# Norms of a one-core fp32 transformer kernel done by halves of the channels, with the first products ordered by high parts

## The chip, the cores and the metric

The kernel is one program on one core of a Trainium2 chip. The metric is the device time of that core in microseconds. The kernel before takes 1885.22 us in the median of 3 runs (1884.35 to 1890.95).

## The reference

Three transformer blocks follow each other on x of 256 tokens by 1024 channels, all in fp32. What matters here:

```python
def rms_norm_2(x, g):
    y = xf * lax.rsqrt(jnp.mean(xf * xf, axis=-1, keepdims=True) + NORM_EPS)
    return (y * g).astype(x.dtype)

def swiglu(x, w_gate, w_up, w_down):
    return (jax.nn.silu(x @ w_gate) * (x @ w_up)) @ w_down

# first block: hybrid mixer ("proj", "w_out"), then a mixture of experts ("moe"), then a final norm
h = h + hybrid_mixer(rms_norm(h, norm1_g), ...)
h = h + hier_moe(rms_norm(h, norm2_g), ...)
x = rms_norm(h, final_norm_g)
# second block, two layers
for layer in range(2):
    x = x + 0.5 * rms_norm_2(swiglu(rms_norm_2(x, g[0]), ...), g[1])    # ffn0, ffn2
    m = mixer_ab(rms_norm_2(x, g[2]), ...) if layer == 0 else mixer_c(rms_norm_2(x, g[2]), ...)
    x = x + rms_norm_2(m, g[3])
    x = x + 0.5 * rms_norm_2(swiglu(rms_norm_2(x, g[4]), ...), g[5])    # ffn1, ffn3
```

## The kernel before, in words

The 256 tokens are two tiles (t = 0 and 1) of 128. All weights come as a stream of 1 MB units through a ring of 5 buffers, loaded by SyncE. A product in full precision is made of three in TensorE's fast fp32 form: the operands are split into a high part and a low part, and high by high, high by low and low by high are summed. ScalarE makes the high part of a weight unit (L814, `split`), VectorE subtracts it to get the low part (L1305, `split`); a wait on `w_lo` holds TensorE until then.

Between two stages stands a norm, for each tile of tokens. For the norm after a stage and the one before the next:

- ScalarE sums the squares of the stage's result in PSUM (L833, L839), GpSimd turns the sums into rp (L723, L715, L716), VectorE multiplies the result by its gain (L1335) and forms the new row X (L1344; L1323 and L1316, L1317 after the mixture of experts).
- F is X times the next gain (L1358). For the stages in `SCALED` (proj, ab, c) it is also multiplied by rn (L1356), for which ScalarE sums the squares of X (L869, `pre_sums`) and GpSimd takes the power (L715, L716). The FFNs apply rn later, in the silu (L1077) and its product (L1798).
- TensorE turns F by 8 transposes a tile (L2186, `x_turn`), ScalarE copies them as the high part h_hi (L882; L880 for ab), VectorE subtracts for the low part h_lo (L1369), and for c also copies them plainly into H (L1372). Each is two instructions, one for each half of the channels.
- The first products: L2633 to L2635 for an FFN (`gate_up`, 24 for a tile, 12 for each weight unit), L2210 for c (`split_tokens`, 24 for a tile and unit), L2716 for ab.

The order of the work is written out by hand on each engine. In an FFN `gate_up(0, 0)` is followed by the turns of tile 1 and `gate_up(0, 1)`; then come the steps s = 1 to 10, each needing two more gate and up units and, one step behind, a down unit. For s = 0 a product waits for h_lo of its half of the channels:

```python
if s == 0:
    pe.wait_ge(S("h_lo"), HI0[name] + 2 * t + j + 1)
for k in range(4):
    pe.matmul(bank[4 + t][:, :], x_hi, w[0][:, k, :], start=first, stop=False)
    pe.matmul(bank[4 + t][:, :], x_hi, w[1][:, k, :], start=False, stop=False)
    ins = pe.matmul(bank[4 + t][:, :], x_lo, w[0][:, k, :], start=False, stop=end)
```

The turns of an FFN's tiles go to PSUM banks 4, 5 and 6, 7 (`turn_bank`); `gate_up` writes banks 4 and 5, the sums of a stage are banks 0 to 3. ffn1 and ffn3 follow a square product (L2951, L2448), in which the turns of tile 0 stand between its quarters. For c, `split_tokens` of two units is done for tile 0, then tile 1; `keep_busy(n)` are n products of constants whose result is not used (L2255; each leaves two records).

## Time and profile before

| | |
|---|---|
| median of 3 runs | 1885.22 us (1884.35 to 1890.95) |
| the profiled execution | 1885.83 us |
| its span | 1884.0 us |
| TensorE busy | 1829.6 us, 97% of the span, 10816 products |
| VectorE busy | 1176.7 us, 62% |
| ScalarE busy | 887.3 us, 47% |
| GpSimd busy | 49.9 us, 3% |
| mean granted TensorE clock | 0.988 of full speed |
| DMA | 363.58 MB, mean 193 GB/s |

The span is what the profile's rows lie in; the execution's time is 1.8 us longer. In the profile's rows PE is TensorE, DVE VectorE, ACT ScalarE, POOL GpSimd, SP SyncE, and L12 is line 12 of the kernel before. The stages lie at these times of the span: proj from 0, the w_out and moe norm at 341 to 362, the experts to 745, ffn0's start at 749 to 763, ab at 936 to 957, ffn1 at 1126 to 1157, ffn2 at 1321 to 1338, c at 1512 to 1545, ffn3 at 1676 to 1707, the last norm at 1871 to 1882.

### The profile page before, as it was taken

To read this page: it belongs to the slowest core of one execution; us is meant where nothing else is said; L and a number is where in the kernel's file an instruction comes from. 1 tells how busy PE (TensorE), PEld (TensorE's weight loads), DVE (VectorE), ACT (ScalarE), POOL (GpSimd) and SP (SyncE) were. 2 spreads that over 40 slices of the span, in tenths; PEclk is the share of its full clock that TensorE was granted. 3 is DMA by queue.
4 is the path that set the end of the run, shared out by engine and by line. 5 is a ranking of instruction groups with operands and counts; after the bars stand their busy time and mean duration, and the time that the engine had idled before them with its cause. 6 is when DMAs were issued, how large, how long until landed. Compare 5 with 4: busy or idle time off the path is not lost.

```text
span 1884.0 us, 25827 instructions
## 1 busy us (share of the span) xinstructions
PE 1829.6 (97%) x10816; PEld 1568.6 (83%) x10816; DVE 1176.7 (62%) x1458; ACT 887.3 (47%) x1091; POOL 49.9 (3%) x107
## 2 busy tenths in 40 slices
PE   7999999999999999999999999999999999999998
PEld 7998889878888887788888898888788889887887
DVE  5345666479898898645468966554645456745454
ACT  4433442367777675544323245444444345535442
POOL 0030000000000000000000000000000010000000
PEclk9989999999999999999999999999999999999999
DMA  8342334479899888555333007544555534226540
GB/s 353 135 157 90 113 112 180 174 291 363 329 351 343 340 338 323 186 193 201 134 116 131 25 3 294 195 177 182 203 190 176 191 135 152 96 98 248 187 176 39
DMA packets 51523, 363.58 MB, mean 193 GB/s; under 512 B 5712, under 2 KB 5840, under 8 KB 8784
## 3 DMA queue, kind: packets, MB, share of 16 engines
q1 hardware_dynamic: 51264, 359.83, 51.3%
q8 instruction: 86, 1.41, 0.3%
q10 hardware_dynamic: 144, 2.10, 0.3%
q14 instruction: 29, 0.24, 0.0%
HBM read 360.86 MB, written 1.05 MB: 192 GB/s over the span
## 4 chain that ended last, share of the span: by engine, by line
PE 87%; DVE 7%; ACT 4%; issue 2%; POOL 0%; DMA 0%; DVEq 0%; SPq 0%; POOLq 0%; ACTq 0%
PE bank L2633 8%; PE bank L2635 8%; PE bank L2634 8%; PE bank L2171 7%; PE bank L2660 4%; PE bank L2658 4%; PE bank L2659 4%; PE bank L2225 4%; PE bank L2525 3%; PE bank L2527 3%; PE bank L2526 3%; PE bank L2210 3%; PE bank L2448 3%; PE bank L2356 3%; PE bank L2540 2%
## 5 line engine op out<-in xcount | busy, mean ns | idle before, releaser
L1305 DVE TENSOR_TENSOR w_a<-ring,w_a 128x2048 fp32r<-128x2048 f32 x221 | 504.2, 2290 | 277.2 <-ACT w_a L814 276.3
L814 ACT ACTIVATE w_a<-ring 128x2048 fp32r<-128x2048 f32 x221 | 420.2, 1912 | 188.2 <-PE bank L2660 90.1
L2633 PE MATMUL bank<-w_a,h 128*128 128x512 f32 x536 | 212.7, 397 | 6.0 <-DVE h L1369 6.0
L2635 PE MATMUL bank<-w_a,h 128*128 128x512 f32 x536 | 209.2, 390 | 0.0
L2634 PE MATMUL bank<-w_a,h 128*128 128x512 f32 x536 | 208.7, 389 | 0.0
L1305 DVE TENSOR_TENSOR w_b<-ring,w_b 128x2048 fp32r<-128x2048 f32 x62 | 142.0, 2291 | 67.8 <-ACT w_b L814 67.1
L2171 PE MATMUL bank<-h,w_a 128*128 128x256 f32 x1088 | 145.8, 289 | 0.7 <-DVE w_a L1305 0.7
L2171 PEld LDWEIGHTS bank<-h,w_a 128*128 128x128 f32 x1088 | 137.8, 196 | 3.5 <-issue 3.2
L814 ACT ACTIVATE w_b<-ring 128x2048 fp32r<-128x2048 f32 x62 | 118.6, 1914 | 45.7 <-PE bank L2660 25.7
L1077 ACT ACTIVATE sil<-bank,tiny 128x256 f32<-128x256 f32 x88 | 41.8, 475 | 175.2 <-PE bank L2635 175.2
L2633 PEld LDWEIGHTS bank<-w_a,h 128*128 128x128 f32 x536 | 100.7, 188 | 27.1 <-DVE h L1369 4.9
L2635 PEld LDWEIGHTS bank<-w_a,h 128*128 128x128 f32 x536 | 100.6, 188 | 21.5
L2634 PEld LDWEIGHTS bank<-w_a,h 128*128 128x128 f32 x536 | 100.8, 188 | 20.0
L2658 PE MATMUL bank<-w_a,hid 128*128 128x512 f32 x264 | 103.2, 391 | 0.0
L2660 PE MATMUL bank<-w_a,hid 128*128 128x512 f32 x264 | 102.8, 389 | 0.0
L2659 PE MATMUL bank<-w_a,hid 128*128 128x512 f32 x264 | 102.7, 389 | 0.0
L2525 PE MATMUL bank<-w_a,xg 128*128 128x512 f32 x244 | 97.9, 401 | 0.9 <-DVE xg L1680 0.9
L2527 PE MATMUL bank<-w_a,xg 128*128 128x512 f32 x244 | 96.0, 393 | 0.0
L2526 PE MATMUL bank<-w_a,xg 128*128 128x512 f32 x244 | 95.7, 392 | 0.0
L800 ACT ACTIVATE arena<-bank 128x512 f32<-128x512 f32 (+2 forms) x51 | 29.1, 571 | 140.6 <-PE bank L2171 56.9
L1798 DVE SCALAR_TENSOR_TENSOR hid<-bank,tiny,sil 128x256 f32<-128x256 f32 x88 | 42.3, 480 | 73.5 <-ACT sil L1077 73.5
L2210 PE MATMUL bank<-w_a,h 128*128 128x256 f32 x672 | 84.5, 287 | 1.4 <-DVE h L1369 1.4
(473 smaller groups left out, 3277.1 us busy)
## 6 DMA issues: line engine op xcount, KB each, us to landing
ring<-in_stream SPq DMA_DIRECT2D x330, 1024.0 KB, 4.9
G<-in_gains SPq DMA_DIRECT2D x15, 512.0 KB, 5.7
cmp_area<-in_cmp_w ACTq DMA_DIRECT2D x1, 2048.0 KB, 10.9
sm<-in_small SPq DMA_DIRECT2D x1, 1582.0 KB, 13.1
con<-in_consts SPq DMA_DIRECT2D x1, 1032.0 KB, 17.1
X<-in_x SPq DMA_DIRECT2D x2, 512.0 KB, 4.9
out_x<-X SPq DMA_DIRECT2D x4, 256.0 KB, 2.0
sm<-in_small SPq DMA_DIRECT2D x1, 730.5 KB, 23.5
```

What stands on the lines that cost most here:

```text
L814: act.activation(w_slot(unit)[:, 0, :], ring[:, unit % RING, :], ACT.Copy).then_inc(S("w_hi"), 1)
L1305: dve.tensor_tensor(w_slot(unit)[:, 1, :], ring[:, unit % RING, :], w_slot(unit)[:, 0, :].bitcast(FP32), ALU.subtract).then_inc(S("w_lo"), 1)
L2171: ins = pe.matmul(ps, w(wp, k), xp[:, k, :], start=(a == 0 and k == 0), stop=(a == 2 and k == terms - 1))
L2525: pe.matmul(bank[4][:, :], x_hi, w[0][:, k, :], start=(half == 0 and k == 0), stop=False)
L2526: pe.matmul(bank[4][:, :], x_hi, w[1][:, k, :], start=False, stop=False)
L2527: ins = pe.matmul(bank[4][:, :], x_lo, w[0][:, k, :], start=False, stop=(half == 1 and k == 3))
L2633: pe.matmul(bank[4 + t][:, :], x_hi, w[0][:, k, :], start=first, stop=False)
L2634: pe.matmul(bank[4 + t][:, :], x_hi, w[1][:, k, :], start=False, stop=False)
L2635: ins = pe.matmul(bank[4 + t][:, :], x_lo, w[0][:, k, :], start=False, stop=end)
L2658: pe.matmul(ps, x_hi, w[0][:, f, d], start=(s == 0 and f == 0), stop=False)
L2659: pe.matmul(ps, x_hi, w[1][:, f, d], start=False, stop=False)
L2660: return pe.matmul(ps, x_lo, w[0][:, f, d], start=False, stop=(s == last and f == 1))
```

## The change

1. **F by halves.** F, and for the FFNs X too, are made in two instructions of 512 channels. The counter `hs` counts halves, and `x_turn` waits for each half before its 4 transposes.
2. **High parts first.** In the first step of an FFN the 8 products that need only h_hi come before the 4 that need h_lo; the first wait is for h_hi. In c the first unit of each tile waits likewise.
3. **Banks.** An FFN's turns go to banks 6, 7 (tile 0) and 0, 1 (tile 1).
4. **The third weight unit** of an FFN is split by ScalarE before the copies of tile 1, and the sum of squares of tile 1's X (`pre_sums`) comes after the first silu.
5. **c's norm** has an order of its own on ScalarE and VectorE (`norms_c`); the first unit's low part is made in two halves around F.
6. **Fewer keep-busy products** in c: 4 and 2 instead of 8 and 8.

```diff
@@ turn_bank
+            if name in FFNS:
+                return half if t else 6 + half
             return (4, 7)[half] if name in BY_TILE else 4 + 2 * t + half
@@ SyncE
-                        sp.wait_ge(S("hs"), 2 * NB[name])
+                        sp.wait_ge(S("hs"), 4 * NB[name])
@@ ScalarE: post_sums (squares(name, t) holds the two sums of squares, L833 and L839)
+                if name == "c":
+                    split("c", 0)
+                    squares(name, 0)
+                    pre_sums(name, 0)
+                    squares(name, 1)
+                    turned_in(name, 0)
+                    split("c", 1)
+                    pre_sums(name, 1)
+                    turned_in(name, 1)
+                    return
...
-                    else:
+                    elif t == 0:
                         turned_in(name, t)
                         pre_sums(name, t)
-                    if of and t == 0 and SPLIT_EARLY[name] < 2:
-                        split(of, 1)
+                    else:
+                        split(name, 2)
+                        turned_in(name, t)
@@ ScalarE: gated
-                split(name, 2)
                 silu(0, 0)
+                pre_sums(name, 1)
                 split(name, 3)
@@ VectorE: rows (was the end of sums_in)
+                for half in range(2):
+                    d = slice(512 * half, 512 * half + 512)
+                    ins = dve.scalar_tensor_tensor(X[:, t, d], F[:, t, d], rp[:, t:t + 1], X[:, t, d], ALU.mult, ALU.add)
+                    renewed(name, t, half, ins)
+
+            def renewed(name, t, half, ins):
+                if half == 0:
+                    half_renewed(ins)
+                    dve.wait_ge(S("x_half"), x_halves[0])
+                else:
+                    ins.then_inc(S("x_new"), 1)
+                    dve.wait_ge(S("x_new"), 2 * (NB[name] - 1) + t + 1)
+                gained_half(name, t, half)
+
+            def gained_half(name, t, half):
...
+                if name in SCALED:
+                    if half == 0:
+                        dve.wait_ge(S("rn"), 2 * NB[name] + t + 1)
+                    ins = dve.scalar_tensor_tensor(F[:, t, d], X[:, t, d], rn[:, t:t + 1], G[:, 1, d], ALU.mult, ALU.mult)
+                else:
+                    ins = dve.tensor_tensor(F[:, t, d], X[:, t, d], G[:, 1, d], ALU.mult)
+                ins.then_inc(S("hs"), 1)
@@ VectorE: c
+            def norms_c():
+                post_gain("c", 0)
+                rows("c", 0)
+                split("c", 0, slice(0, UNIT // 2))
+                gained("c", 0)
+                split("c", 0, slice(UNIT // 2, UNIT))
+                low_in("c", 0)
+                post_gain("c", 1)
+                split("c", 1)
+                rows("c", 1)
+                whole_in("c", 0)
+                gained("c", 1)
+                low_in("c", 1)
+                whole_in("c", 1)
@@ TensorE: x_turn
-                pe.wait_ge(S("hs"), 2 * NB[name] + t + 1)
                 for half in range(2):
+                    pe.wait_ge(S("hs"), 4 * NB[name] + 2 * t + half + 1)
@@ TensorE: split_tokens(..., first=False)
+                        if first and a != 1:
+                            pe.wait_ge(S("h_lo" if a else "h_hi"), HI0[name] + 2 * t + 2)
@@ TensorE: gate_up
                         if s == 0:
+                            pe.wait_ge(S("h_hi"), HI0[name] + 2 * t + j + 1)
+                            for k in range(4):
+                                x_hi = h_hi[:, 4 * j + k, t * P:(t + 1) * P]
+                                pe.matmul(bank[4 + t][:, :], x_hi, w[0][:, k, :], start=(j == 0 and k == 0), stop=False)
+                                pe.matmul(bank[4 + t][:, :], x_hi, w[1][:, k, :], start=False, stop=False)
                             pe.wait_ge(S("h_lo"), HI0[name] + 2 * t + j + 1)
-                        for k in range(4):
+                            for k in range(4):
+                                ins = pe.matmul(bank[4 + t][:, :], h_lo[:, 4 * j + k, t * P:(t + 1) * P], w[0][:, k, :],
+                                                start=False, stop=(j == 1 and k == 3))
+                        for k in range(4) if s else ():
@@ TensorE: c
-            pe.wait_ge(S("h_lo"), HI0["c"] + 2)
             for n in range(2):
-                split_tokens(group_begin(f"c{8 + n}"), "c", n, range(0, 1))
-            keep_busy(8)
+                split_tokens(group_begin(f"c{8 + n}"), "c", n, range(0, 1), n == 0)
+            keep_busy(4)
             x_turn("c", 1)
-            keep_busy(8)
-            pe.wait_ge(S("h_lo"), HI0["c"] + 4)
+            keep_busy(2)
             for n in range(2):
-                split_tokens(bank[5 + GI[f"c{8 + n}"] % 2], "c", n, range(1, 2))
+                split_tokens(bank[5 + GI[f"c{8 + n}"] % 2], "c", n, range(1, 2), n == 0)
```

VectorE's order at the norm of c, with the semaphores that each instruction waits for. F<-bank,G is the result times its gain, X<-F,tiny,X the new row, F<-X,tiny,G the row for the turns, w_a<-ring,w_a a low part of weights, h<-bank,h is h_lo, H<-bank the plain copy. Before:

```order
1048 L1344 SCALAR_TENSOR_TENSOR X<-F,tiny,X 128x1024 [waits s_rp,s_fg]
1049 L1305 TENSOR_TENSOR w_a<-ring,w_a 128x2048 [waits s_w_hi,s_x_new]
1050 L1356 SCALAR_TENSOR_TENSOR F<-X,tiny,G 128x1024 [waits s_rn,s_gain1]
1051 L1369 TENSOR_TENSOR h<-bank,h 128x4x128 [waits s_h_hi] x2
1052 L1372 COPY H<-bank 128x4x128 x2
1053 L1305 TENSOR_TENSOR w_a<-ring,w_a 128x2048 [waits s_w_hi]
1054 L1335 TENSOR_TENSOR F<-bank,G 128x512 [waits s_ss_p,s_gain0]
1055 L1335 TENSOR_TENSOR F<-bank,G 128x512 [waits s_ss_p]
1056 L1344 SCALAR_TENSOR_TENSOR X<-F,tiny,X 128x1024 [waits s_rp,s_fg]
1057 L1356 SCALAR_TENSOR_TENSOR F<-X,tiny,G 128x1024 [waits s_rn,s_x_new]
```

The same place in the changed kernel, whose line numbers are its own:

```order
1066 L1382 SCALAR_TENSOR_TENSOR X<-F,tiny,X 128x1024 [waits s_rp,s_fg]
1067 L1322 TENSOR_TENSOR w_a<-ring,w_a 128x1024 [waits s_w_hi,s_x_new]
1068 L1411 SCALAR_TENSOR_TENSOR F<-X,tiny,G 128x512 [waits s_rn,s_gain1,s_dve_chain]
1069 L1411 SCALAR_TENSOR_TENSOR F<-X,tiny,G 128x512
1070 L1322 TENSOR_TENSOR w_a<-ring,w_a 128x1024 [waits s_w_hi]
1071 L1431 TENSOR_TENSOR h<-bank,h 128x4x128 [waits s_h_hi] x2
1072 L1368 TENSOR_TENSOR F<-bank,G 128x512 [waits s_ss_p,s_gain0]
1073 L1368 TENSOR_TENSOR F<-bank,G 128x512 [waits s_ss_p]
1074 L1322 TENSOR_TENSOR w_a<-ring,w_a 128x2048 [waits s_w_hi]
1075 L1382 SCALAR_TENSOR_TENSOR X<-F,tiny,X 128x1024 [waits s_rp,s_fg]
1076 L1436 COPY H<-bank 128x4x128 [waits s_x_new]
1078 L1411 SCALAR_TENSOR_TENSOR F<-X,tiny,G 128x512 [waits s_rn]
```

The low part of the first unit stands in two pieces around F, and the low part of the second unit has moved behind the gain of tile 1; the plain copies of tile 0 have moved behind X of tile 1.

ScalarE at the start of ffn2: sums of squares of the result (junk,tiny<-bank), high parts of the turned rows (h<-bank), sum of squares of X (junk,tiny<-X), high parts of weights (w_a, w_b<-ring), the silu. Before, then changed:

```order
645 L833 ACTIVATE junk,tiny<-bank 128x512 [waits s_half_sums]
646 L839 ACTIVATE junk,tiny<-bank 128x512 [waits s_unit_used]
647 L882 ACTIVATE h<-bank 128x4x128 [waits s_x_turned] x2
648 L869 ACTIVATE junk,tiny<-X 128x1024 [waits s_x_new]
649 L814 ACTIVATE w_b<-ring 128x2048 [waits s_unit_used,s_unit1]
650 L1077 ACTIVATE sil<-bank,tiny 128x256 [waits s_gu_0,s_rn]
```

```order
645 L830 ACTIVATE junk,tiny<-bank 128x512 [waits s_half_sums]
646 L836 ACTIVATE junk,tiny<-bank 128x512 [waits s_unit_used]
647 L816 ACTIVATE w_b<-ring 128x2048 [waits s_unit_used,s_unit1]
648 L899 ACTIVATE h<-bank 128x4x128 [waits s_x_turned] x2
649 L1094 ACTIVATE sil<-bank,tiny 128x256 [waits s_gu_0,s_rn]
650 L886 ACTIVATE junk,tiny<-X 128x1024 [waits s_x_new]
```

The third unit's high part has moved ahead of the copies of tile 1, and the sum of squares of X behind the silu.

## Rows read from the trace of the kernel before

**Rows 1.** The page: busy time of each engine, and the chain that ended last
```profile
PE 1829.6 (97%) x10816; PEld 1568.6 (83%) x10816; DVE 1176.7 (62%) x1458; ACT 887.3 (47%) x1091; POOL 49.9 (3%) x107
...
PE 87%; DVE 7%; ACT 4%; issue 2%; POOL 0%; DMA 0%; DVEq 0%; SPq 0%; POOLq 0%; ACTq 0%
```
**Rows 2.** Waits of TensorE: us in total, times, longest us
```profile
PE bank L2186 <- DVE F L1356: 13.4, 5, 8.3
PE bank L2633 <- DVE h L1369: 6.0, 6, 1.1
```
**Rows 3.** VectorE's instructions: duration ns min/median/max by tile; one by the timeline
```profile
L1358 DVE TENSOR_TENSOR F<-X,G x10: 1224/1225/1227, 342.0 to 1694.7; 128x1024 f32<-128x1024 f32 x10
L1341 DVE SCALAR_TENSOR_TENSOR X<-F,tiny,X x4: 744/748/752, 1874.7 to 1880.8; 128x512 f32<-128x512 f32 x4
...
224.64 0.69 DVE L1576 TENSOR_TENSOR SQ<-SQ,arena 128x512 f32<-128x512 f32 x1
```
**Rows 4.** Timeline, ffn2's start: start us, us, instruction [idle before <-releaser]
```profile
1327.91 1.03 PE L2186 MATMUL bank<-con,F 128*128 128x128 f32 x8
1329.17 1.29 DVE L1369 TENSOR_TENSOR h<-bank,h 128x512 fp32r<-128x512 f32 x2 [1.94 <-ACT h L882]
1330.01 0.47 PE L2633 MATMUL bank<-w_a,h 128*128 128x512 f32 x1 [1.07 <-DVE h L1369]
1333.16 1.28 DVE L1344 SCALAR_TENSOR_TENSOR X<-F,tiny,X 128x1024 f32<-128x1024 f32 x1 [0.52 <-POOL tiny L716]
...
1337.82 0.50 PE L2633 MATMUL bank<-w_a,h 128*128 128x512 f32 x1 [0.98 <-DVE h L1369]
```
**Rows 5.** Timeline, ffn0's tile 1
```profile
762.58 0.50 PE L2633 MATMUL bank<-w_a,h 128*128 128x512 f32 x1 [0.97 <-DVE h L1369]
```
**Rows 6.** Timeline, ffn1's tile 1 and its fourth weight unit
```profile
1145.90 1.09 PE L2186 MATMUL bank<-con,F 128*128 128x128 f32 x8
1147.97 0.50 PE L2633 MATMUL bank<-w_a,h 128*128 128x512 f32 x1 [0.98 <-DVE h L1369]
...
1154.15 2.29 DVE L1305 TENSOR_TENSOR w_b<-ring,w_b 128x2048 fp32r<-128x2048 f32 x1 [0.90 <-ACT w_b L814]
...
1156.49 0.50 PE L2633 MATMUL bank<-w_b,h 128*128 128x512 f32 x1
```
**Rows 7.** Timeline, c's norm and first products
```profile
1515.51 2.29 DVE L1305 TENSOR_TENSOR w_a<-ring,w_a 128x2048 fp32r<-128x2048 f32 x1
1516.75 1.13 POOL L715 TENSOR_SCALAR tiny<-tiny 128x1 f32<-128x1 f32 x1 [2.66 <-ACT junk L869]
...
1519.96 1.97 PE L2186 MATMUL bank<-con,F 128*128 128x128 f32 x8 [2.39 <-DVE F L1356]
1523.34 7.38 PE L2210 MATMUL bank<-w_a,h 128*128 128x256 f32 x48 [1.41 <-DVE h L1369]
...
1530.48 0.22 POOL L715 TENSOR_SCALAR tiny<-tiny 128x1 f32<-128x1 f32 x1 [2.78 <-ACT junk L869]
...
1531.44 1.28 DVE L1356 SCALAR_TENSOR_TENSOR F<-X,tiny,G 128x1024 f32<-128x1024 f32 x1 [2.23 <-POOL tiny L716]
...
1535.45 6.01 PE L2210 MATMUL bank<-w_a,h 128*128 128x256 f32 x48
```
**Rows 8.** Stretches: busy us of PE, PEld, DVE, ACT, POOL; PEclk, DMA share, GB/s
```profile
755.00:765.00 10.00, 8.25 (x39) 6.41 (x38) 4.47 (x6) 4.95 (x7) 2.12 (x5) 1.00 0.32 104
945.00:950.00 5.00, 4.30 (x24) 4.31 (x25) 2.58 (x3) 2.35 (x7) 0.98 (x3) 0.66 0.01 3
1520.00:1526.00 6.00, 4.59 (x20) 4.19 (x21) 4.10 (x5) 4.15 (x7) 0.40 (x1) 0.50 0.32 134
```
**Rows 9.** Timeline, the turns of proj (tile 1), moe (tile 1) and ab (tile 0)
```profile
11.21 1.97 PE L2186 MATMUL bank<-con,F 128*128 128x128 f32 x8 [1.00 <-DVE F L1356]
...
357.96 1.09 PE L2186 MATMUL bank<-con,F 128*128 128x128 f32 x8 [0.41 <-DVE F L1358]
...
943.86 1.09 PE L2186 MATMUL bank<-con,F 128*128 128x128 f32 x8 [1.51 <-DVE F L1356]
```

More of the change, by code:

```diff
@@ L1299, in link, with split, half_renewed @@
                 dve.wait_ge(S("dve_chain"), chain[0])
-            def split(name, n):
+            def split(name, n, part=slice(0, UNIT)):
                 unit = D_UNITS[name] + n
                 dve.wait_ge(S("w_hi"), SPLIT0[name] + n + 1)
-                dve.tensor_tensor(w_slot(unit)[:, 1, :], ring[:, unit % RING, :], w_slot(unit)[:, 0, :].bitcast(FP32),
-                                  ALU.subtract).then_inc(S("w_lo"), 1)
+                ins = dve.tensor_tensor(w_slot(unit)[:, 1, part], ring[:, unit % RING, part], w_slot(unit)[:, 0, part].bitcast(FP32),
+                                        ALU.subtract)
+                if part.stop == UNIT:
+                    ins.then_inc(S("w_lo"), 1)
+                else:
+                    link(ins)
+            x_halves = [0]
+            def half_renewed(ins):
+                x_halves[0] += 1
+                ins.then_inc(S("x_half"), 1)
             def sums_in(name, t):
@@ L1361, in turned_in, with low_in @@
+            def gained(name, t):
+                for half in range(2):
+                    gained_half(name, t, half)
             def turned_in(name, t):
+                if name != "ab":
+                    low_in(name, t)
+            def low_in(name, t):
                 tok = slice(t * P, (t + 1) * P)
@@ L1637, in norms @@
                 for t in range(TT):
[L1638 to L1639 removed]
+                    if of and t < SPLIT_EARLY[name]:
                         split(of, t)
                     sums_in(name, t)
[L1642 to L1643 removed]
                     if name == "moe":
@@ L1647, in norms @@
                     elif name != "end":
-                        gained(name, t)
+                        if name in SCALED:
+                            gained(name, t)
                         turned_in(name, t)
-                    if of and t == 0 and SPLIT_EARLY[name] < 2:
-                        split(of, 1)
             dve.wait_ge(S("merged"), 12)
@@ L2202, in split_channels, with split_tokens @@
                 ins.then_inc(S("unit_used"), 1)
-            def split_tokens(ps, name, n, ts=range(TT)):
+            def split_tokens(ps, name, n, ts=range(TT), first=False):
                 w = split_ready(name, n)
```

83 lines of the change are left out of this document (41 added, 42 removed).

## Prediction

> **What bounds the kernel.** I read the page's shares first: TensorE is busy for 97% of the span and holds 87% of the chain that ended last [rows 1]. So only work that keeps TensorE waiting, or runs it at half clock, is worth anything. The table of waits on TensorE comes next: its largest entries are the two that this change aims at, the transposes waiting for VectorE's gained rows (F), and the first FFN products waiting for the low part h_lo [rows 2]. Together they are some 20 us, 1% of the span, and that caps the change. Then I read the timeline around each norm, and the granted clock beside it. A measurement of this kernel can tell about 0.5% (9.4 us) from no change.
>
> **Prices of pieces.** A 1024-wide F takes 1.225 us, a 512-wide X with its pointer scalar 0.748, and a 512-wide tensor_tensor, which F is without a scalar, 0.69 [rows 3]. A whole X takes 1.28 [rows 4]. So X and F of one tile by halves take 0.75+0.69+0.75+0.69, less some 0.16 for the overlap of the unwaited step, plus two waits on itself of 0.04: about 2.86 against 1.28+0.04+1.22 = 2.54. The last F half ends 0.3 us later than F did, the first half 1.1 us earlier. These sizes are known to 0.1; the range takes 0.2.
>
> **ffn2 (the pattern of all FFN starts).** Tile 0: its 8 transposes start at 1327.91, when the products before them end, h_lo's first half starts at 1329.17 when h_hi's is there, and the first product starts at 1330.01, 0.15 after h_lo's first half [rows 4]. With the high parts first the product waits for h_hi: 1329.17+0.12, so it starts at 1329.29, 0.7 earlier; 8 products of 0.226 us cover h_lo. But what follows isn't TensorE's: the second tile's X starts at 1333.16 as before (ScalarE squares it behind the same work), so its F halves are ready at 1333.16+0.75+0.04+0.69 = 1334.64 and 1333.16+2.86 = 1336.02. TensorE is free at 1329.29+5.57 = 1334.86 (the 24 products with their slow first one), turns half 0, waits, turns half 1 from 1336.07 to 1336.6 (8 took 1.03 [rows 4]), and the first product of tile 1 may start there, since h_hi's first half landed by 1336.2. Before it started at 1337.82 [rows 4]. **Term: -1.2.** Tile 0's 0.7 is inside it, not added.
>
> **ffn0.** The same sum, and the chain before it starts 0.25 us earlier, because h_lo of tile 0 is done that much sooner and the rest of VectorE's queue follows: 1.2+0.25. The product of tile 1 would start at 761.1 instead of 762.58 [rows 5]. **-1.45.**
>
> **ffn1, ffn3.** Tile 0 is turned inside the square product, which hides its h_lo already: no gain. Tile 1 of ffn1: F was ready just before the turns at 1145.90, its half 1 is now ready at 1146.17, but half 0 is turned first, from 1145.85 to 1146.4, so nothing waits; h_hi's first half lands 1.3 after the start of the turns (as 1329.17 against 1327.91), the product starts at 1147.25 instead of 1147.97 [rows 6]: -0.7. ScalarE now splits the third unit before it copies h_hi, and VectorE subtracts it right behind h_lo, about 2 us sooner than before. There, the fourth unit's low part ended at 1156.44 and the product waited for it until 1156.49, 0.33 behind its place [rows 6]; that goes. **-1.05 each, -2.1.** The moved norm sum (1.06+0.2 us on ScalarE) now stands behind the first silu; its result is wanted by the second silu only, about 3 us later, so it costs nothing; if that cover were gone it would cost 1.3.
>
> **The c mixer.** Before: GpSimd's first step of the norm took 1.13 us beside VectorE's split of 2.29, though the same step for tile 1 takes 0.22; it ended at 1517.88, the split at 1517.80. The turns follow at 1519.96 after 2.4 us of idle, the first products at 1523.34 [rows 7]. Now only half the split (1.225, as any 1024-wide tensor_tensor) stands there, ending at 1516.73. The Trainium skill, page "SBUF — State Buffer", section "SBUF: two separate sides", says that a VectorE instruction with two SBUF inputs and a GpSimd one exclude each other for the whole instruction. By that rule the step is short again.
> I take the step as held up by the split, since both ended together, and short behind the half split; were it long for another reason, the term below would be 0.9 smaller.
> Chain now: GpSimd done 1517.62, F half 0 at 1518.45, half 1 at 1519.1, second half of the split 1520.2, h_hi's halves at 1519.8 and 1520.4. The products start at 1520.45, 2.9 sooner. 24 of them later (2.9 us at 0.122) comes a **new wait**: the second unit's low part stands behind h_lo and the F of tile 1 (1521.5+1.28) and takes 2.29, to 1525.0, so TensorE idles 1.7 us. Then 24 more products to 1527.9, 4 keep-busy ones (8 records at 0.122) to 1528.9. Tile 1: X 1525.0 to 1526.3, its sum and GpSimd to 1528.4 (VectorE sat idle 2.23 for them before 1531.44), F halves to 1529.25 and 1529.9, turned by 1530.45, two keep-busy products, h_hi at 1531.3: start 1531.35 against 1535.45 [rows 7]. The 10 keep-busy products dropped are in that; kept, they would cost up to 1.5 here. The plain copies of tile 0 now stand behind X, which costs nothing while the norm sum runs beside them. **-4.1.** Of it 1.4 is clock: the first 48 products took 7.2 us, the second 48 5.85, since the granted clock was 0.50 from 1520 to 1526 [rows 7, 8]. Now the pauses ahead are 1.0 and 0.8 us. If the clock still falls, the wait for the second unit hides most of the loss.
>
> **Others.** proj: the second tile's turns begin with F half 0, 0.55 sooner than 11.21 [rows 9], and the splits follow them: -0.5. ab: half 1 is turned 0.35 sooner: -0.35; nothing at tile 1. moe: TensorE waits 0.41 for F, but then for VectorE's f_lo and h_route, pushed back by the longer F: +0.15 [rows 9]. SyncE's waits for the counters only change their number; its gain loads come 0.3 later, and the unit loads behind them have several units in the ring to hide that. Transposes in banks 6, 7, 0, 1 instead of 4 to 7 add no wait: those banks were read long before.
>
> **Sum**: -1.2-1.45-2.1-4.1-0.5-0.35+0.15 = -9.55 us. All of it is TensorE's path; nothing behind it is bound by DMA, since the same units are in the ring. The profiled execution took 1885.83 (span 1884.0), which gives 1876.3; the median of the runs is 0.6 lower, so **1875.6 us**, 0.51% faster.
>
> **Rivals.**
> *The c term is given back.* The new wait of 1.7 us for the second unit is as long as the pause of ab at which the clock fell (1.51 [rows 9]; clock 0.66 over 945 to 950 [rows 8]). If it falls there, the 24+4 products behind run at 0.21: +2.5, and the GpSimd lock is no lock: +0.9. For: both pauses are in this trace. Against: ffn0's second start, with 0.8 and 1.0 us around its turns, kept the full clock [rows 8]. -9.55+3 gives 1878.6. Chance 0.22.
> *More than the sum.* ab's clock doesn't fall, its pauses being 0.3 us shorter: the clock of 0.66 over 5 us is 3.4 us at half speed [rows 8], 1.7 lost, of which some lay in the pause; -1.4 more: 1874.2. Chance 0.14.
> *The halves bring nothing*, because the waits of h_hi and of the second F half take their place (F by halves ends 0.3 later, four FFNs, and no 0.7): about -4.5 is left, from c and the third unit: 1880.7. For: tile 1 of ffn0 and ffn2 does wait for F. Against: the row of h_hi is 0.7 ahead of h_lo. Chance 0.10.
> *Slower*: the clock falls at the FFN starts. The turns now come in two pieces with a pause, 0.9 and 0.75 us, between products. At c it fell for 6 us [rows 8], which costs up to 3. If it does so at all four FFNs: +12-9.55 = +2.45, 1887.7. It decides this way if a stretch of about 3 us with only turns in it is enough; before, ffn0 had one just as long, ending at 762.58 [rows 5], at full clock [rows 8]. Beside that: the page "TensorE: Matmul & The Clock Gate", section "HAM oscillation — how this bites in real kernels", of the Trainium skill tells of small pauses between groups of products that bring the clock down again and again; this trace shows the full clock at ffn0. Chance 0.05.
>
> **Numbers.** The forecast itself holds 0.49: 1874.5 to 1877.2, by the unknown F half (0.2 each), the lock and the start of proj. 8 in 10 with the rivals near it: 1873 to 1880.5. The forecast lies on the 0.5% line (1875.8), so half of it and all of "more" count as faster: 0.44; same 0.53, slower 0.03.
>
> **What would show it.** In the changed trace: FFN products starting behind h_hi, about 1.35 us after the turns; ffn1's and ffn3's fourth unit without a wait; in c GpSimd's step at 0.22, the first products 3 us after the last ones of ffn2, one wait of 1.7 us for the low weights, and a granted clock of 1.00 through 1520 to 1530. Wrong it would be if the clock fell in new places, if the first products still waited for h_lo, or if the DMA queue ended a wait of the splits.

## The result and the profile after

The changed kernel takes 1871.03 us in the median of 4 runs (1869.42 to 1872.72), beside 1887.72 for the kernel before in 4 runs. The ratio is 0.9911, interval 0.989 to 0.9932: faster by 0.9%, where 0.51% was forecast. The profiled executions are 1885.83 and 1871.74 us, their spans 1884.0 and 1870.0. The forecast, 1875.6 with 1873.0 to 1880.5, was 4.6 us too high, and the time lies outside its range.

The page after, busy time and the chain that ended last (compare [rows 1]):

```profile
PE 1822.6 (97%) x10796; PEld 1561.8 (84%) x10796; DVE 1180.4 (63%) x1483; ACT 888.3 (48%) x1091; POOL 51.7 (3%) x107
...
PE 88%; DVE 6%; ACT 3%; issue 2%; POOL 0%; DMA 0%; DVEq 0%; SPq 0%; POOLq 0%; ACTq 0%
```

20 records are gone (10 keep-busy products), yet TensorE's busy time fell by 7.0 us. 20 records of 0.122 are 2.4; the rest is products that no longer run at half clock. The other half of the 14 us is waits. The table of waits on TensorE (engine, line, releaser: us in total, times, longest), against [rows 2]:

```profile
PE bank L2262 <- DMA con<-in_consts: 8.0, 1, 8.0
PE bank L2262 <- DVE F L1413: 3.1, 5, 0.9
PE bank L2262 <- DVE F L1411: 2.6, 3, 1.0
PE bank L2288 <- DVE w_a L1322: 1.3, 1, 1.3
PE bank L2288 <- ACT h L899: 1.1, 2, 0.8
PE bank L2710 <- ACT h L899: 0.8, 3, 0.3
```

The 13.4 us on F of proj, ab and c are 8.0 (the start, now put down to a DMA) and 2.6. The 6.0 on h_lo at six FFN tiles are 0.8 on h_hi at three. The waits for F of moe and the FFNs rose a little, from 2.4 us in 3 to 3.1 in 5. New is the 1.3 on a low part of weights, L1322, in c. The DMA queue ends three waits of ScalarE's splits, 3.0 us in all (the longest, 2.5, at 19 us of the span, in proj); before it ended two, 2.3 us in all. None of them is at the norm of an FFN, of ab or of c, so this sign of being wrong came only where it had been before.

The two traces were laid over each other at the turns (the transposes) and first products of each stage; the differences add up to 14.1 us, as the two profiled executions differ (1885.83 and 1871.74):

| place | forecast | measured | how read (before, after) |
|---|---|---|---|
| proj, first product | -0.5 | -0.64 | 18.08, 17.44 |
| proj, later | 0 | -1.45 | clock, see e2, e8, e13 |
| moe | +0.15 | -0.08 | second logits 359.93, 357.76 |
| ffn0, tile 1's first product | -1.45 | -1.63 | 762.58, 758.75, less 2.20 at its start |
| ab, first product | -0.35 | -0.45 | 945.70, 941.42 |
| ab, its 64 products | 0 | -1.63 | clock |
| ffn1 | -1.05 | -1.23 | turns of ffn1 to those of ffn2 |
| ffn2 | -1.2 | -1.41 | to its last product, 1517.19, 1508.68 |
| c | -4.1 | -4.32 | to the turns of ffn3, 1682.59, 1669.76 |
| ffn3 | -1.05 | -1.26 | from its turns to TensorE's last product, 1877.73, 1863.64 |

ffn2's start after, by the timeline, against [rows 4]:

```profile
1320.81 1.04 PE L2262 MATMUL bank<-con,F 128*128 128x128 f32 x8
1322.18 0.47 PE L2710 MATMUL bank<-w_a,h 128*128 128x512 f32 x1 [0.34 <-ACT h L899]
1326.05 0.75 DVE L1388 SCALAR_TENSOR_TENSOR X<-F,tiny,X 128x512 f32<-128x512 f32 x1 [0.52 <-POOL tiny L718]
...
1328.98 0.66 PE L2262 MATMUL bank<-con,F 128*128 128x128 f32 x4 [0.63 <-DVE F L1413]
1329.39 0.47 PE L2710 MATMUL bank<-w_a,h 128*128 128x512 f32 x1
```

From the turns to the first product 1.37 us (forecast 1.38), from X to tile 1's first product 3.34 (forecast 3.44, before 4.66). The second half of F ends the wait, as forecast. Two things were a little better. F's second half overlaps X's (0.08 each time). And X of tile 1 starts 5.24 us after the first turns, where it was 5.25, so nothing was lost ahead of it.

The fourth unit at ffn1, against [rows 6]:

```profile
1141.27 0.50 PE L2710 MATMUL bank<-w_a,h 128*128 128x512 f32 x1 [0.25 <-ACT h L899]
...
1146.37 2.29 DVE L1322 TENSOR_TENSOR w_b<-ring,w_b 128x2048 fp32r<-128x2048 f32 x1 [1.24 <-ACT w_b L816]
...
1149.56 0.39 PE L2719 MATMUL bank<-w_b,h 128*128 128x512 f32 x1
```

The low part ends at 1148.66, 0.9 us ahead of its product; before, the low part ended at 1156.44, and this product and the next came 0.33 us late (1156.49 and 1156.83 behind one at 1156.04, where products follow each other by 0.23).

The norm of c, against [rows 7]:

```profile
1507.00 1.23 DVE L1322 TENSOR_TENSOR w_a<-ring,w_a 128x1024 fp32r<-128x1024 f32 x1
1508.24 0.22 POOL L717 TENSOR_SCALAR tiny<-tiny 128x1 f32<-128x1 f32 x1 [2.66 <-ACT junk L886]
1510.03 1.32 PE L2262 MATMUL bank<-con,F 128*128 128x128 f32 x8 [0.97 <-DVE F L1411]
1512.13 3.10 PE L2288 MATMUL bank<-w_a,h 128*128 128x256 f32 x24 [0.78 <-ACT h L899]
1516.51 3.10 PE L2288 MATMUL bank<-w_a,h 128*128 128x256 f32 x24 [1.28 <-DVE w_a L1322]
1519.72 1.42 DVE L1411 SCALAR_TENSOR_TENSOR F<-X,tiny,G 128x512 f32<-128x512 f32 x2 [0.84 <-POOL tiny L718]
1522.63 5.99 PE L2288 MATMUL bank<-w_a,h 128*128 128x256 f32 x48 [0.33 <-ACT h L899]
```

GpSimd's step takes 0.22 behind the half split. With the 8.51 us put back by which ffn2 ends sooner, the first products start at 1520.64 (forecast 1520.45), the new wait is 1.28 (forecast 1.7), tile 1's products start at 1531.14 (forecast 1531.35). The 24 products take 3.10, so this stretch is at full clock.

ab's first products after (timeline), and the stretch of its granted clock (columns as in [rows 8]):

```profile
939.41 1.32 PE L2262 MATMUL bank<-con,F 128*128 128x128 f32 x8 [0.97 <-DVE F L1411]
```
```profile
940.00:945.00 5.00, 4.30 (x37) 4.00 (x37) 2.46 (x4) 2.35 (x6) 0.98 (x3) 1.00 0.01 3
945.00:950.00 5.00, 4.70 (x43) 4.46 (x41) 1.80 (x5) 1.85 (x4) 0.95 (x4) 1.00 0.00 0
```

Where it was 0.66 [rows 8], it is 1.00. So of the miss of 4.5 us between forecast and trace, 3.1 are clock falls that are not there, at ab and in proj, and the rest, not quite 1.5, lies in small differences of eight terms.

### The profile page after: what moved, and what is told of

It is laid out like the page before. It is cut to its first block, busy times and chain, and to the rows that moved or that the text cites. A ratio compares the mean times of both kernels' runs of the same rounds, so it can differ in the third digit from the quotient of the medians.

```text
span 1870.0 us, 25816 instructions
## 1 busy us (share of the span) xinstructions
PE 1822.6 (97%) x10796; PEld 1561.8 (84%) x10796; DVE 1180.4 (63%) x1483; ACT 888.3 (48%) x1091; POOL 51.7 (3%) x107
## 3 DMA queue, kind: packets, MB, share of 16 engines
q8 instruction: 86, 1.41, 0.3%
HBM read 360.86 MB, written 1.05 MB: 194 GB/s over the span
## 4 chain that ended last, share of the span: by engine, by line
PE 88%; DVE 6%; ACT 3%; issue 2%; POOL 0%; DMA 0%; DVEq 0%; SPq 0%; POOLq 0%; ACTq 0%
PE bank L2721 8%; PE bank L2719 8%; PE bank L2720 8%; PE bank L2247 7%; PE bank L2746 4%; PE bank L2744 4%; PE bank L2745 4%; PE bank L2288 4%; PE bank L2303 4%; PE bank L2603 3%; PE bank L2605 3%; PE bank L2604 3%; PE bank L2526 3%; PE bank L2434 3%; PE bank L2618 2%; PE bank L2620 2%
## 5 line engine op out<-in xcount | busy, mean ns | idle before, releaser
L1322 DVE TENSOR_TENSOR w_a<-ring,w_a 128x2048 fp32r<-128x2048 f32 (+1 forms) x222 | 504.4, 2280 | 271.9 <-ACT w_a L816 271.0
L2719 PE MATMUL bank<-w_a,h 128*128 128x512 f32 x472 | 186.7, 396 | 0.0
L2721 PE MATMUL bank<-w_a,h 128*128 128x512 f32 x472 | 184.2, 390 | 0.0
L1322 DVE TENSOR_TENSOR w_b<-ring,w_b 128x2048 fp32r<-128x2048 f32 x62 | 142.1, 2291 | 66.6 <-ACT w_b L816 65.9
L2720 PE MATMUL bank<-w_a,h 128*128 128x512 f32 x472 | 183.7, 389 | 0.0
L2721 PEld LDWEIGHTS bank<-w_a,h 128*128 128x128 f32 x472 | 88.6, 188 | 18.8
L2720 PEld LDWEIGHTS bank<-w_a,h 128*128 128x128 f32 x472 | 88.7, 188 | 17.6
L2719 PEld LDWEIGHTS bank<-w_a,h 128*128 128x128 f32 x472 | 88.7, 188 | 17.4
```

Of the source, the lines that this page charges most:

```text
L1322: ins = dve.tensor_tensor(w_slot(unit)[:, 1, part], ring[:, unit % RING, part], w_slot(unit)[:, 0, part].bitcast(FP32), ALU.subtract)
```

## The experiments

Theories: the program's terms, stage by stage, are right, and the parts work as I said; or some part does nothing, or another's work. Rival for the rest: the clock falls belong to pauses that the change shortens, or they are chance. All stages are compared between the turns and products named above. "Loss" is the sum of (1 - granted clock) x 5 us over stretches of 5 us; it is the time that a fall would cost if every product in it were on the path, so it is an upper bound. Each run but e8, e11, e12 and e16 was also timed against the kernel before:

| run | ratio to before | run | ratio to before |
|---|---|---|---|
| e1 | 0.9924 (0.9896 to 0.9952) | e7 | 0.9939 (0.9922 to 0.9956) |
| e2 | 0.9933 (0.9912 to 0.9955) | e9 | 0.9941 (0.9915 to 0.9968) |
| e3 | 0.9939 (0.9923 to 0.9956) | e10 | 0.9937 (0.9917 to 0.9956) |
| e4 | 0.9945 (0.9929 to 0.9962) | e13 | 0.9922 (0.9904 to 0.9941) |
| e5 | 0.9935 (0.9918 to 0.9952) | e14 | 0.9927 (0.9907 to 0.9946) |
| e6 | 0.9967 (0.9955 to 0.9978) | e15 | 0.9980 (0.9965 to 0.9994) |

The intervals are as wide as most effects in question, so the verdicts rest on the stages.

**e1**, the changed kernel, F of ab whole:
```diff
             def gained(name, t):
+                if name == "ab":
...
+                    dve.scalar_tensor_tensor(F[:, t, :], X[:, t, :], rn[:, t:t + 1], G[:, 1, :], ...).then_inc(S("hs"), 2)
+                    return
                 for half in range(2):
```


> The changed kernel with F of the ab stage made whole again (proj, c and the FFNs stay in halves). Theory 1 (the pause sets the clock): in the changed kernel TensorE paused 0.97 us before ab's first turns and the granted clock stayed 1.00, in the kernel before it paused 1.51 and the clock fell to 0.5 for some 3.4 us. Here the pause is 1.5 again, so the clock falls again, the first 64 products of ab take 8.9 to 9.1 us instead of 7.4, and the stage ends 1.9 to 2.3 us later than in the changed kernel. Theory 2 (the fall at ab was a matter of where in time the stage lay, not of the pause): the clock stays 1.00, only the 0.45 us of the later turns comes back.


The stage ended 0.5 us later and the clock stayed 1.00: 9.15 us from the first turns to the second (9.25 in the changed kernel, 10.71 before). Theory 2. The median was 1870.29.

**e2**, the same edit for proj.


> The changed kernel with F of proj made whole again. The first products start 0.64 us later (18.08 instead of 17.44). Theory 1 (the clock's fall at 100 us of the kernel before hung on where in time its 128x24 products lay): the fall comes back, the products at 100 to 106 take twice their time, and by 127 us the kernel is 3 to 3.7 us behind the changed one, of which some 1.5 comes back by 185. Theory 2 (that fall had another cause, or comes by chance): no fall at 100, 0.64 us and no more.


First products at 17.96, 0.52 later. This is less sure than it looks: in the 13 profiles with proj's F in halves they start between 17.44 and 17.95, in the four of the kernel before (e11 among them) between 18.02 and 18.09, so the halves are worth 0.5 us in the mean. The fall at 100 us came back, with the same clocks as before (0.50, then 0.85), and at the moe turns the kernel was 2.0 us behind. That fits theory 1. But e1, whose proj is that of the changed kernel, also fell at 100 (0.68 over 5 us). Over all profiles it fell there in 5 of 5 with proj's F whole and in 7 of 13 with it in halves. So the place is prone to a fall, and these counts lean to the change as help without settling it.

**e3**, the first step of an FFN waits for h_lo again:
```diff
                         if s == 0:
-                            pe.wait_ge(S("h_hi"), HI0[name] + 2 * t + j + 1)
...
                             pe.wait_ge(S("h_lo"), HI0[name] + 2 * t + j + 1)
-                        for k in range(4) if s else ():
+                        for k in range(4):
```


> The changed kernel in which the first step of an FFN waits for h_lo again before its first product and mixes high and low parts as before (c keeps its order). Theory 1 (the order of the products gives 0.65 us at a tile's start, tile 0 hidden where tile 1 waits for F): from the turns of tile 1 to its first product 0.65 more in each of four FFNs, in all 2.4 to 3.0 us more than the changed kernel. Theory 2 (the halves of X and F give the gain, the order nothing): under 0.5 us.


ffn0 +0.3, ffn1 +0.73, ffn2 +1.12, ffn3 +0.70: 2.85 us, theory 1. At ffn0's tile 1 the order is worth nearly nothing: F's second half puts half 1 of the turns at 758.06 in e3, and h_lo's half 0 is there at 758.69, when these turns are done.

**e4**, X and F of the FFNs whole:
```diff
...
+                if name in FFNS:
...
+                    dve.tensor_tensor(F[:, t, :], X[:, t, :], G[:, 1, :], ALU.mult).then_inc(S("hs"), 2)
+                    return
                 for half in range(2):
                     gained_half(name, t, half)
```


> The changed kernel with X and F of the four FFNs made whole again, high parts still first. Theory 1 (the gain at ffn0 and ffn2 is 0.65 for the order and 0.7 for the halves): from X's start to the first product of tile 1 3.9 to 4.0 us instead of 3.33, so ffn0 and ffn2 lose 0.6 us each, ffn1 and ffn3, whose F is covered, 0 or win 0.2: in all 1.0 to 1.3. Theory 2 (the halves cost as much as they give, because the last half of F ends 0.3 later): 0 within 0.3.


ffn0 1.03 (counted from the sum into X), ffn2 0.75, ffn1 0.22, ffn3 0.22: 2.2 us. (The edit makes X whole too; those lines are not shown.) From X of tile 1 to its product at ffn2 it took 4.02 instead of 3.34, as theory 1 says. The rest of ffn0 comes through tile 0, which holds up tile 1's X by another 0.34. Theory 1 with a size too small.

**e5**, c's norm in the old order:
```diff
                 post_gain("c", 0)
                 rows("c", 0)
-                split("c", 0, slice(0, UNIT // 2))
+                split("c", 0)
                 gained("c", 0)
-                split("c", 0, slice(UNIT // 2, UNIT))
                 low_in("c", 0)
+                whole_in("c", 0)
+                split("c", 1)
                 post_gain("c", 1)
-                split("c", 1)
                 rows("c", 1)
-                whole_in("c", 0)
```
(On ScalarE the sums of squares of tile 1, `squares(name, 1)`, stand behind `split("c", 1)` again.)


> The changed kernel with c's norm in the order of before on ScalarE and VectorE (whole split of the first unit ahead of F, plain copies of tile 0 ahead of the second unit's split); halves, order of products and keep-busy products stay as changed. Theory 1 (the order is worth 1.06 us for GpSimd's step, which waits for the whole split, and 1.28 for the copies ahead of tile 1's X): GpSimd's step takes 1.13 again, and from the last product of ffn2 to tile 1's first product it is 2.0 to 2.5 us longer than the 13.95 of the changed kernel, without counting the clock. If the clock falls at the pause ahead of the turns, up to 1 more shows at tile 1. Theory 2 (the pieces of the low part only move a wait): under 0.7.


c took 2.03 us more, 0.88 of it at the first turns: theory 1. The timeline of e5, VectorE's split and GpSimd's step beside it:

```profile
1507.13 2.29 DVE L1322 TENSOR_TENSOR w_a<-ring,w_a 128x2048 fp32r<-128x2048 f32 x1
```
```profile
1508.37 1.13 POOL L717 TENSOR_SCALAR tiny<-tiny 128x1 f32<-128x1 f32 x1 [2.66 <-ACT junk L886]
```

With a whole split the step takes 1.13 and ends just behind it (1509.50, 1509.42), with half of one 0.22. That agrees with what the Trainium skill says in "SBUF — State Buffer", section "SBUF: two separate sides", of the two engines excluding each other. The clock did not fall at c in e5, though the pause ahead of the turns was 1.85 us and the one behind them 0.78.

**e6**, the third unit late, and the sum of squares of X ahead of the first silu again:
```diff
-                        split(name, 2)
                         turned_in(name, t)
+                        pre_sums(name, t)
...
+                split(name, 2)
                 silu(0, 0)
-                pre_sums(name, 1)
                 split(name, 3)
```


> The changed kernel with the third unit split by ScalarE behind the copies of tile 1 and the sum of squares, as before. Theory 1 (it pays only where the fourth unit's low part was waited for): 0.3 us each at ffn1 and ffn3, 0 at ffn0 and ffn2, 0.6 in all. Theory 2 (with products that start earlier, the third and fourth units are wanted earlier, so undoing it costs at all four): 0.7 each, 2.8 in all.


Both theories were too low: 1.18 at ffn0, 1.10 at ffn1, 1.09 at ffn2, 1.07 at ffn3, 4.4 in all. The timeline of e6 at ffn2:

```profile
1338.88 1.05 ACT L886 ACTIVATE junk<-X 128x1024 bf16<-128x1024 f32 x1
...
1339.92 1.91 ACT L816 ACTIVATE w_b<-ring 128x2048 fp32r<-128x2048 f32 x1
...
1341.86 2.29 DVE L1322 TENSOR_TENSOR w_b<-ring,w_b 128x2048 fp32r<-128x2048 f32 x1 [2.15 <-ACT w_b L816]
...
1344.07 0.48 DVE L1874 SCALAR_TENSOR_TENSOR hid<-bank,tiny,sil 128x256 f32<-128x256 f32 x1
...
1344.61 0.50 PE L2719 MATMUL bank<-w_b,h 128*128 128x512 f32 x1 [0.79 <-DVE hid L1874]
```

Step 1's first product needs the bank that VectorE empties into hid, and hid stands on VectorE behind the third unit's low part (1341.86 to 1344.15). A product that starts a microsecond sooner finds that queue late. But the edit puts back two things, and the rows don't part them: the split of the third unit stands behind the sum of squares, which takes ScalarE from 1338.88 to 1339.92. By an estimate from these rows, with the sum behind the silu all of this would come some 1.0 us sooner, which is more than the wait of 0.79. So the 4.4 us belong to the pair, the third unit's place and the moved sum; what each is worth without the other was not run.

**e15**, e3 and e4 together, so that of the FFN parts only the third unit's place, with the moved sum, and the banks are left:


> The changed kernel with X and F of the FFNs whole and the order of products as before, so that of the FFN parts the third unit's earlier split and the banks are left. Undone one by one, order, halves and third unit cost 2.8, 2.2 and 4.4 us, 9.4 together, where the FFN starts gained only 5.4 in all. Theory 1 (the third unit's place is worth little by itself, 0.33 at ffn1 and ffn3, and as much as 1.1 a stage only where the products start early): the FFN stages lose 4.4 to 5.0 against the changed kernel. Theory 2 (the third unit's place is worth 4.4 by itself): they lose about 1.


ffn1 lost 0.95, ffn2 1.48, ffn3 0.94, together 3.4 of the 3.9 us that these three had gained. ffn0 lost 1.75 up to tile 1's first product, counted from the keep-busy products (36 records) ahead of it; the clock fell only behind it, and again at ab. In all this is 5.1 us, a little over the range of theory 1 and far from theory 2: alone, the third unit's place with the moved sum is worth 0.28 at ffn1, 0.31 at ffn3 and nothing at the other two. Timed, this kernel was 0.2% faster than the one before (0.998, 0.9965 to 0.9994).

**e7**, `keep_busy(8)` twice:


> The changed kernel with 8 and 8 keep-busy products in c instead of 4 and 2. Theory 1 (they stand on TensorE's path): tile 1's turns start 0.9 us later (4 more of 0.24) and its first product 2.1 us later than in the changed kernel (10 more of 0.24, less the 0.33 that it waited). Theory 2 (they stand in time that is idle anyway): under 0.5.


Turns of tile 1 +0.71, its product +1.20. The ten products are on the path, but eight of them take 1.78 us, not 1.95, and some stood in the pause for h_hi. Theory 1, though it had the size at nearly twice the measured one.

**e8 and e16**, the kernel before again, and **e13**, the changed kernel again:


> The kernel before, profiled once more. Theory 1 (a fall of the clock at a given place is partly chance from run to run): the falls at 100 and at 945 us, which cost 3.2 and 1.7 us in the profiled execution of before, don't both come again, while a stage's times at full clock agree within 0.1. Theory 2 (the program's pauses fix every fall): both come again, within 1 us of the same place.

> The kernel before, a third profile. Theory 1 (at c the fall belongs to the program, at ab and 100 us it is chance): c falls again, 3 to 3.6 us lost between 1510 and 1530; at ab and 100 us either. Theory 2 (all of them belong to the program): c, ab and 100 all fall.

> The changed kernel once more, in five rounds. Outside c, the clock lost 19.0, 16.2 and 15.6 us in three profiles of kernels built on the one before, and 13.4 to 19.5 in those built on the changed one. Theory 1 (outside c the falls are chance of the run): this profile again loses 13 to 20 us to the clock, its span less that loss is 1853 to 1854.5, and where the falls lie differs from the first profile. Theory 2 (the change itself keeps the clock up outside c): the loss is under 15 again, and the falls lie where they lay.

| loss to the clock, us | before | e8 | e16 | changed | e13 |
|---|---|---|---|---|---|
| 85 to 120 | 3.4 | 1.7 | 1.7 | 0 | 1.75 |
| 120 to 175 | 8.55 | 6.85 | 6.85 | 10.25 | 6.8 |
| 350 to 390 | 5.15 | 5.1 | 1.7 | 5.1 | 5.1 |
| ab | 1.7 | 1.7 | 0 | 0 | 0 |
| 1030 to 1105 | 0 | 0 | 1.7 | 0 | 0 |
| c | 3.4 | 3.45 | 3.4 | 0 | 0 |
| all | 22.2 | 18.8 | 15.35 | 15.35 | 13.65 |
| span | 1884.0 | 1881.1 | 1879.8 | 1870.0 | 1868.7 |
| span less loss | 1861.8 | 1862.3 | 1864.5 | 1854.7 | 1855.1 |

A last fall comes in all five behind TensorE's last product (1863.64 in the changed kernel, where the clock fell at 1869), and is left out, since nothing waits for it. (e13's expectation counted it, 1.5 us: so read, the loss is 15.15 and the span less loss 1853.6, both in theory 1's range.)

e8 by itself spoke for its theory 2, as both falls came again, the one at 100 us at half its size. e16 took ab's away, which is e16's theory 1: c fell in each profile of the kernel before, ab did not. The stretches of c in e16:

```profile
1515.00:1520.00 5.00, 2.47 (x14) 2.23 (x15) 3.62 (x6) 3.35 (x6) 0.00 (x0) 0.72 0.49 200
1520.00:1525.00 5.00, 5.00 (x29) 5.00 (x28) 4.45 (x4) 1.17 (x5) 2.03 (x3) 0.60 0.38 121
```

In e11 the loss was 3.4 too: 4 of 4. With the changed c a fall came in e6 and e15, 1.7 us each, and in nine other profiles not. That fall is the program's. The others move about: two of the same kernel's three profiles fell at ab. The spans of the two kernels differ by 12.3 us in the mean: 8.0 with all losses taken off, 3.4 at c, 0.9 outside it. Outside c the losses of these profiles are nearly the same (15.4 and 14.5), so theory 1 of e13 holds for them. e13's median was 1870.01.

The loss at c is not its price. In e16 the fall lies in the 48 products (8.37 us instead of 6.0), and yet F of tile 1 is ready at 1528.00 and TensorE only at 1528.61, so without the fall the turns could have started 0.6 us sooner at most. In the kernel before, slower turns (1.97 for 1.09) hold up VectorE's chain, and by the same comparison the price is 0.8: an estimate, from where F is ready behind ffn2's last product, 15.53 us there and 14.82 in e16. And with the changed c the fall costs nothing. This is e15's row, at half clock from 1525.8 to 1529.2:

```profile
1525.38 7.48 PE L2297 MATMUL bank<-w_a,h 128*128 128x256 f32 x48 [0.78 <-ACT h L899]
```

The 48 products run on without the wait of 1.28, and the keep-busy products behind them start 7.32 us after the first, as in the changed kernel (1512.13, 1519.45). c is 161.11 us long in e15, 161.09 in e6 and 161.08 in the changed kernel. That is what the prediction said of this case: the wait for the second unit hides the loss.

**e11 and e12**, ab's pause again, in the kernel before with F of ab in halves, and e1 repeated:


> The kernel before with F of ab alone in halves. Before this, ab's clock fell in both profiles of the kernel before (pause 1.51 ahead of the turns), in none of seven with F in halves (0.97), and not in the one with F whole (1.5) at another time. Theory 1 (the longer pause is needed for the fall): no fall at ab, from its first turns to its second 9.2 us instead of 10.7. Theory 2 (it hangs on the stage's place in time, or other parts of the change): it falls again, 10.2 or more.

> The changed kernel with F of ab whole, once more. Theory 1 (a pause of 1.5 makes a fall likely, not sure): from ab's first turns to its second 9.2 us in this one or 10.7, either can come, and the earlier profile (9.2) was the lucky one of three. Theory 2 (something else in the changed kernel keeps the clock up): 9.2 again.


e11 9.25 us from turns to turns, e12 9.15: no fall in either. With the pause of 1.5 us ab fell in 2 of 5 profiles (before and e8 yes, e16, e1 and e12 no), with F in halves in 1 of 13 (e15). That leans to the shorter pause as protection, and does not prove it.

**e10**, nine keep-busy products in the pause at 125 us:
```diff
             def compress_halves():
+                keep_busy(9, 4)
                 ps = side_begin("hid_halves")
```


> The changed kernel with 9 keep-busy products (2.2 us) in the 2.37 us pause ahead of the 64 products of 36 columns at 127 us, behind which the clock is 0.50 for 14 us in every trace so far. Theory 1 (the pause makes the clock fall): it stays 1.00, the 64 products take half of their 12.9 us, and 6 to 8 us are gained. Theory 2 (narrow products make it fall, as at 100 us in the kernel before, where no pause stood before 128x24 products): the fall comes all the same, within 3 us of where it was, and the gain is under 1.5.


The 64 narrow products of the changed kernel, then those of e10, and e10's stretches:

```profile
127.13 12.89 PE L2386 MATMUL bank<-arena,cmp_area 128*128 128x36 f32 x64 [2.37 <-DVE arena L1499]
```
```profile
127.53 9.51 PE L2387 MATMUL bank<-arena,cmp_area 128*128 128x36 f32 x64 [0.36 <-DVE arena L1499]
```
```profile
128.00:130.00 2.00, 2.00 (x20) 2.00 (x20) 0.61 (x1) 0.00 (x0) 1.83 (x4) 1.00 0.21 82
130.00:135.00 5.00, 5.00 (x36) 5.00 (x35) 0.00 (x0) 0.00 (x0) 1.51 (x3) 0.73 0.00 0
135.00:140.00 5.00, 5.00 (x25) 5.00 (x25) 0.91 (x5) 0.00 (x0) 0.00 (x0) 0.50 0.00 0
```

The pause is 0.36 and the clock still falls, after 130 us, in the midst of the narrow products, with TensorE busy throughout. By the moe turns 2.9 us were gained, between the two theories, but e12, without the edit, gained 2.6 there by chance. Theory 2 for the cause; the median, 1871.22, is that of the changed kernel.

**e9 and e14**, c's second unit in parts, a try at a kernel that beats both:
```diff
                 post_gain("c", 1)
-                split("c", 1)
                 rows("c", 1)
                 whole_in("c", 0)
                 gained("c", 1)
                 low_in("c", 1)
+                split("c", 1)
...
+            some_of_c(ps_0, 0, 0, (0, 1, 2), True, True)
+            some_of_c(ps_1, 1, 0, (0, 2), True, False)
             keep_busy(4)
             x_turn("c", 1)
+            some_of_c(ps_0, 0, 1, (0, 1, 2), True, True)
+            some_of_c(ps_1, 1, 0, (1,), False, True)
+            some_of_c(ps_1, 1, 1, (0, 2, 1), True, True)
```
(`some_of_c` issues for one unit and one tile the products high by high (0), low weights by high (1) and high weights by low (2), with the waits that each needs.)


> The changed kernel, and in c the second unit's products that need no low part of the weights come first, its low part is made behind h_lo of tile 1, and X of tile 1 ahead of it; TensorE turns tile 1 between. The wait of 1.28 us for the second unit's low part should go, F of tile 1 be ready some 2 us sooner. Theory 1 (VectorE's queue sets c): tile 1's turns start at about 8.3 us behind c's first turns instead of 10.5, and c's first 96 products end 1.5 to 2.0 us sooner than in the changed kernel. Theory 2 (TensorE's pauses make the clock fall here): gain lost, up to 2 us more.

> The version with c's second unit in parts, timed beside the changed kernel in the same job. Its stage c was 1.1 us shorter in its one profile. Theory 1 (that gain is real, and small beside the clock's chance): c 1.0 to 1.2 us shorter again, medians within 3 us of the changed kernel's, on either side. Theory 2 (its pauses bring falls of their own at c or behind): a fall between 1510 and 1540 us, and a median over 2 us worse.


From turns to turns 8.43, and c 1.12 and 1.13 us shorter in the two profiles: real, and less than the 1.5 to 2.0 that e9 expected, since F of tile 1 now ends a wait of 0.89. No fall at c. The medians were 1873.31 in e9 and 1871.91 in e14, the latter timed beside 1870.01 for the changed kernel. The mean granted clock of the eleven runs gives a loss of 18.0 us, beside 14.2 in ten runs of the changed kernel, more than the stage gains. So the microsecond does not show in the time, and this is no better kernel; whether its pauses bring those falls or chance does is open.

## Why the prediction was right and wrong

- **The bound** was right: the gain that the stages explain came out of TensorE's waits and half-clock stretches at the norms.
- **The FFN terms** were right in mechanism and 0.18 to 0.21 too small each (1.45, 1.05, 1.2, 1.05 forecast; 1.63, 1.23, 1.41, 1.26 measured). The one for the moe norm had the wrong sign, +0.15 for -0.08. Together with proj, ab and c these are the small differences, not quite 1.5 us.
- **The third unit** was put at 0.33 at ffn1 and ffn3 and called free elsewhere. e15 confirms the 0.3 when it is alone. What the sum did not say is that the other FFN terms stand on it and on the moved norm sum: without the two e6 gives 4.4 of the 5.5 us back. I had named the silu as cover of the moved sum, not what becomes late when the products start sooner.
- **c** was right in its total and its mechanism: order 2.0 (e5), fewer keep-busy products 1.2 (e7, forecast up to 1.5), GpSimd's step short behind the half split (0.22 for 1.13), the new wait of 1.28. These overlap, so they don't sum to 4.32 by themselves. One piece was too large: the 1.4 of clock within it. Tile 1's turns waited for F, not for the slow products, and the estimate above gives 0.6 to 0.8. So some of the closeness of 4.1 to 4.32 is luck.
- **The step that failed is the clock outside c.** The forecast took 1.4 us of clock into c and held the fall at ab, and those in proj, for fixed, so that outside c the clock stood in the sum at nothing. ab's was in the rival "more than the sum", with 0.14; proj's was in no case. In the pair of traces these two gave 3.1 of the 14.1 us. In the runs, 45 of the kernel before and 10 of the changed one, the means are 1885.5 and 1870.5, 15.0 us apart. The table by stages explains 11.0 of them (9.55 forecast); the other 4.0 agree with what the granted clocks of the same runs show outside c, below.
- **The range** had no term for the clock from run to run. The loss varied from 15.35 to 22.2 us in three profiles of one kernel, nearly the width of the whole range of 7.5. The before that the sum started from had the largest loss of the three. Two slips don't carry the miss: the first rival names +2.5 and +0.9 and adds 3, and "half of it and all of more" is 0.49/2 + 0.14 = 0.385, not 0.44.
- **Open** is why the clock fell less outside c. The mean granted clock was 0.9885 in the 45 runs of the kernel before and 0.9924 in the 10 of the changed one, 21.7 and 14.2 us of loss. c explains 3.4 of these 7.5. The rest goes along with the FFN starts. Between ffn0's start and TensorE's last product, outside c, the eight profiles with the FFN starts of the changed kernel and c not in parts (changed, e13, e1, e12, e2, e5, e7, e10) have no fall; e9 and e14 have one of 3.4 us near 1090; the four with an FFN part undone lose 3.4 (e3, e4) and 5.1 (e6, e15), the four of the kernel before 1.7 each. The timed runs say the same: a loss of 15.4 us in the mean of 33 runs of the first group, 18.0 in 11 of the second, 20.5 in 26 of the third. This is also why the medians of e3, e4, e6 and e15 lie 5.6, 5.8, 9.1 and 11.0 us above the changed kernel's mean, twice what the stages lost or more (2.85, 2.2, 4.4, 5.1). Which pause or start does it no run shows, and since e9 and e14 have the changed kernel's program up to c, chance is in it too.
- The rivals: "given back" and "the halves bring nothing" did not come. The clock did not fall at any FFN start of the changed kernel; in e15, with X and F whole and the products in the order of before, it did once at ffn0.

## What to carry to other kernels

When a change makes a chain start sooner, ask for each queue behind it how long it had been early. The part of a change that seems worth a third of a microsecond can be what lets the others pay, and only undoing each part, and one alone, tells this. Before taking one profile's half-clock stretches as fixed, compare two or three profiles of the same kernel: a fall that comes each time belongs in the sum, at what it delays on the path and not at its whole loss (0.6 to 0.8 us for 3.4 here), and the others belong in the range. And when an edit that undoes a part puts back two things, as e6 does, name both.

## What the hardware showed beside what was expected

The granted clock falls without a pause. In the kernel before it fell at 99.7 us, 3.0 us into products of 24 columns, and in e10 at 132.3 us among products of 36 columns, 4.8 us behind a pause of 0.36 us, TensorE busy in both. The Trainium skill, "TensorE: Matmul & The Clock Gate", section "HAM oscillation — how this bites in real kernels", tells it of waits between groups of products; c, with pauses of 2.39 and 1.41 us around its turns, is of that kind, these two stretches are not. (The small pauses that the prediction quotes from it stand in the section behind, "A second HAM failure mode: psum-queue depth-cycling".) Where it falls, outside c, differs between executions of one program.

GpSimd's small step was held up in a new place, beside the third unit's split at ffn2 of the changed kernel:

```profile
1331.76 1.51 POOL L717 TENSOR_SCALAR tiny<-tiny 128x1 f32<-128x1 f32 x1 [5.81 <-ACT junk L886]
```

Its result is wanted by the second silu at 1335.20, and is there at 1333.91, so it costs nothing.
